# Normalising and rounding a token tile on VectorE instead of ScalarE, in the first stage of a hybrid attention kernel

## The chip, the core and the metric

The kernel runs on one core of a Trainium2 chip. The metric is the device time of one launch, in microseconds (us). The core's engines work side by side and are held together by semaphores only: TensorE (PE in the profile) for matrix products, VectorE (DVE), ScalarE (ACT), GpSimd (POOL), and SyncE (SP), which here issues the transfers.

## The reference

One layer of a diffusion backbone: 2048 sample tokens and 256 prompt tokens of width 1024, all in fp32. Every token is normalised and modulated, then projected into two mixers; their joined output is projected back, and a gated feed-forward follows.

```
h = modulate(rms_norm(x, n1), sh1, sc1)          # rms_norm: x * rsqrt(mean(x*x) + EPS) * g
qg, kg, vg, og, lr, qa, ka, va = split(h @ w_in)
o_gla = gated linear attention, forward and backward, of qg, kg, vg with gates from lr
qa, ka = rms_norm(qa, q_g), rms_norm(ka, k_g)    # and a 2-D rotary for the sample tokens
o_att = softmax attention, 8 query heads on 2 key heads, over tokens and a cache
x = x + g1 * (concat(o_gla, o_att) @ w_out)
x = x + g2 * swiglu(modulate(rms_norm(x, n2), sh2, sc2))
y = rms_norm(x, final_g)
```

## The kernel before

The kernel is a row of stages with a barrier between them: modulation parameters, `attention_projection` (names begin with `qkv_`, some 49 to 329 us), `attention` (to about 1205 us), three stages of the gated linear attention, the output projection, and the feed-forward (from about 2040 us). The change touches the class `Front`, which only `attention_projection` uses.

Every fp32 product is done as three products of halves: a value is copied in the rounded form fp32r (`hi`), the rest is `value - hi` (`lo`), and `split_product` adds hi·hi, hi·lo and lo·hi.

`attention_projection` goes over 18 tiles of 128 tokens. `steps` runs a software pipeline: in step u, `U.at(d)` gives tile u-d, and each engine does its pieces of that step in the order in which its `step` function lists them. An instruction waits with `wait_ge` on the count of a semaphore; the engine goes on with nothing else meanwhile. The path of a tile:

- `load` (SP) brings tile u as `qkv_x`, 128 x 1024. It waits for the transposes of tile u-2.
- `squares` (ACT, L255) squares and sums it. `mean` (DVE, L260) makes mean + EPS, one element per partition; `root` (POOL, L270) raises it to the power -0.5; `normalise` (ACT, L265) multiplies the tile by it, in place. All four are of tile u.
- `transpose` (PE, L277) is of tile u-1. `modulate` (ACT, L288, eight instructions) writes `qkv_hT`; `high` (ACT, L302) writes the rounded copy `qkv_hi`, `low` (DVE, L307) writes `qkv_lo`. `keep` (SP) stores `qkv_hT` for later stages.
- The products of tile u-2 with the weights (PE, 48 matrix instructions) wait for `low`.
- Of tile u-3: ACT copies the results out of PSUM (L438, L440) and squares them (L444); DVE sums the squares per head (L483, the first of its instructions in a step) and adds EPS (L485); POOL makes the root of ten elements (L533); DVE scales (L493), multiplies by a table (L499), POOL by another (L539, two instructions), DVE adds them (L502), rounds (L505, L506) and takes the rests (L508, L510).
- Of tile u-4: PE transposes the halves (L556, L558); ACT copies them out (L452, L455).

POOL's order in a step is: the two tables `qkv_cs` for tile u-3 (L530, L531: gains times rotary table, 128 x 640 each, both inputs in SBUF), L533, L539, and last `root` of tile u. Its tables for step u+1 have no input that is late, so they follow `root` of step u directly. ACT's order is: L438, L440, L444, then L452, L455, then `squares`, `modulate`, `high`, `normalise`. DVE's order is: L483 to L510, `mean`, `low`.

The weights of the stage are split once, in step 1 (L324 on ACT, L329 on DVE), behind that step's pieces.

Of the kernel before, what the change touches and what calls it, by code (L numbers as in the profile page):

```python
# [10 lines left out]
ALU = mybir.AluOpType  # L11
ACT = mybir.ActivationFunctionType
# [33 lines left out]
def wait(eng, sem, value):  # L46

    if not (isinstance(value, int) and value <= 0):
        eng.wait_ge(sem, value)
# [19 lines left out]
def steps(eng, depth, body):  # L69

    first = (depth + 2) // 2
    for u in range(2 * first):
        body(Step(u // 2, u % 2, True))
    with eng.Fori(first, N_LAT // 2) as i:
        for par in range(2):
            body(Step(i, par, False))
    for u in range(N_LAT, NT + depth):
        body(Step(u // 2, u % 2, True))
# [6 lines left out]
def bc(ap, axis, n):  # L85

    a = ap.unsqueeze(axis)
    shape = list(a.shape)
    shape[axis] = n
    return a.to_broadcast(shape)  # L90
# [137 lines left out]
class Front:  # L228
# [25 lines left out]
        wait(act, self.s.sq, t)  # L254
        act.activation(self.junk[:, :], self.x[:, par, :], ACT.Square, accum_out=self.ss[:, par, :]).then_inc(self.s.sq, 1)  # L255

    def mean(self, dve, T):
        t, half, par = T
        dve.wait_ge(self.s.sq, t + 1)
        dve.tensor_scalar(self.ms[:, par, :], self.ss[:, par, :], 1.0 / D_MODEL, EPS, ALU.mult, ALU.add).then_inc(self.s.ms, 1)  # L260

    def normalise(self, act, T):
        t, half, par = T
        act.wait_ge(self.s.rstd, t + 1)
        act.activation(self.x[:, par, :], self.x[:, par, :], ACT.Copy, scale=self.rstd[:, par, :]).then_inc(self.s.xn, 1)  # L265

    def root(self, pool, T):
        t, half, par = T
# [26 lines left out]
        sp.wait_ge(self.s.hT, t + 1)  # L295
        sp.dma_start(self.g.hT_tile(t), self.hT[:, par].rearrange("p k q -> p (k q)")).then_inc([self.s.kept0, self.s.kept1][par], 16)

    def high(self, act, T):
        t, half, par = T
        act.wait_ge(self.s.hT, t + 1)  # L300
        wait(act, self.used, t - 1)
        act.activation(self.hi[:, par], self.hT[:, par], ACT.Copy).then_inc(self.s.hi, 1)  # L302

    def low(self, dve, T):
        t, half, par = T
        dve.wait_ge(self.s.hi, t + 1)
        dve.tensor_tensor(self.lo[:, par], self.hT[:, par], self.hi[:, par].bitcast(F32), ALU.subtract).then_inc(self.s.split, 1)  # L307

# [33 lines left out]
def constant_parts(dve, parts):  # L342

    dve.memset(parts[:, :, 3, 1:HD].bitcast(F32), 0.0)
    dve.memset(parts[:, :, 3, 0:1].bitcast(F32), -1.0)


def attention_projection(nc, g):

    NH = AH + KVH  # L350
    with ExitStack() as stack:
# [5 lines left out]
        fr = Front(ph, s, g, 0, s.mkv)  # L357
# [25 lines left out]
        def key_tile(t):  # L383

            return t + 2 if cond_of(t) else t

        with nc.Block() as block:
# [41 lines left out]
            @block.scalar  # L429
            def _(act):  # L430

                def step(U):
                    if T := U.at(3):
                        t, hf, par = T
                        act.wait_ge(s.mq, t + 1)

                        wait(act, s.vlo, t - 1)
                        act.activation(qkv[:, par, 0:NQ], p_q[par][:, :], ACT.Copy).then_inc(s.eq, 1)  # L438
                        act.wait_ge(s.mkv, t + 1)
                        act.activation(qkv[:, par, NQ:D_ATT], p_kv[:, 0:D_ATT - NQ], ACT.Copy).then_inc(s.ekv, 1)  # L440
                        act.wait_ge(s.ekv, t + 1)
                        act.wait_ge(s.eq, t + 1)
                        wait(act, s.ssh, t)
                        act.activation(psq[:, :], qkv[:, par, 0:NH * HD], ACT.Square).then_inc(s.psq, 1)  # L444
                    if T := U.at(4):
                        t, hf, par = T
                        act.wait_ge(s.ptr, t + 1)
                        if isinstance(t, int) and t < 2:
                            pass
                        else:  # L450
                            act.wait_ge([s.qout0, s.qout1][par], hf * 16)
                        act.activation(qT[:, par], p_t[:, 0:AH * P].rearrange("p (h q) -> p h q", h=AH), ACT.Copy).then_inc(s.eptr, 1)  # L452
                        kt = key_tile(t)
                        col = kt * P
                        act.activation(g.keysT[:, :, :, bass.ds(col, P)],  # L455
                                       p_t[:, AH * P:(AH + 4) * P].rearrange("p (g a q) -> p g a q", g=KVH, a=2), ACT.Copy).then_inc(s.eptk, 1)
                    if T := U.at(0):
                        fr.squares(act, T)
                    if T := U.at(1):
                        fr.modulate(act, T)  # L460
                        fr.high(act, T)
                    if T := U.at(0):
                        fr.normalise(act, T)
                    if U.first(1):
                        w_act(act)

                steps(act, 4, step)
                act.wait_ge(s.eptk, NT)

            @block.vector  # L470
            def _(dve):
                constant_parts(dve, khl)
                dve.wait_ge(s.gain, 16 * 10)
                for n in range(2):
                    dve.tensor_scalar(gain[:, n, 0:AH, :], bc(gsrc[:, n, :], 1, AH), HD ** -0.5, None, ALU.mult)
                    last = dve.tensor_copy(gain[:, n, AH:NH, :], bc(gsrc[:, 2 + n, :], 1, KVH))
                last.then_inc(s.gmul, 1)

                def step(U):
                    if T := U.at(3):  # L480
                        t, hf, par = T
                        dve.wait_ge(s.psq, t + 1)
                        dve.tensor_reduce(ssh[:, :], psq[:, :].rearrange("p (h d) -> p h d", d=HD), AX.X, ALU.add).then_inc(s.ssh, 1)  # L483
                        dve.wait_ge(s.ssh, t + 1)
                        dve.tensor_scalar(msh[:, :], ssh[:, :], 1.0 / HD, EPS, ALU.mult, ALU.add).then_inc(s.msh, 1)  # L485

                        vt = key_tile(t)
                        src = qkv[:, par, NH * HD:D_ATT].rearrange("p (g d) -> p g d", g=KVH)
                        dve.wait_ge(s.ekv, t + 1)
                        v_here = g.vals[:, bass.ds(vt * KVH, KVH), :]  # L490
                        dve.tensor_copy(v_here[:, :, 0:HD], src).then_inc(s.vhi, 1)
                        dve.wait_ge(s.rsh, t + 1)
                        dve.tensor_tensor(qn[:, :, :], qkv[:, par, 0:NH * HD].rearrange("p (h d) -> p h d", d=HD),  # L493
                                          bc(rsh[:, :], 2, HD), ALU.mult).then_inc(s.qn, 1)
                        dve.wait_ge(s.vhi, t + 1)
                        dve.tensor_tensor(v_here[:, :, HD:2 * HD], src, v_here[:, :, 0:HD].bitcast(F32), ALU.subtract).then_inc(s.vlo, 1)
                        dve.wait_ge(s.qn, t + 1)
                        dve.wait_ge(s.cs, t + 1)
                        dve.tensor_tensor(m1[:, :, :], qn[:, :, :], cs[:, 0], ALU.mult).then_inc(s.m1, 1)  # L499
                        dve.wait_ge(s.m1, t + 1)  # L500
                        dve.wait_ge(s.m2, t + 1)
                        dve.tensor_tensor(rot[:, par], m1[:, :, :], m2[:, :, :], ALU.add).then_inc(s.rot, 1)  # L502
                        dve.wait_ge(s.rot, t + 1)
                        wait(dve, s.ptr, t)
                        dve.tensor_copy(qhl[:, :, 0, :], rot[:, par, 0:AH, :]).then_inc(s.hq, 1)  # L505
                        dve.tensor_copy(khl[:, :, 0:2, :], bc(rot[:, par, AH:NH, :], 2, 2)).then_inc(s.hk, 1)  # L506
                        dve.wait_ge(s.hq, t + 1)
                        dve.tensor_tensor(qhl[:, :, 1, :], rot[:, par, 0:AH, :], qhl[:, :, 0, :].bitcast(F32), ALU.subtract).then_inc(s.lo_q, 1)  # L508
                        dve.wait_ge(s.hk, t + 1)
                        dve.tensor_tensor(khl[:, :, 2, :], rot[:, par, AH:NH, :], khl[:, :, 0, :].bitcast(F32), ALU.subtract).then_inc(s.lo_k, 1)  # L510
                    if T := U.at(0):
                        fr.mean(dve, T)
                    if T := U.at(1):
                        fr.low(dve, T)
                    if U.first(1):
                        w_dve(dve)

                steps(dve, 4, step)

            @block.gpsimd  # L520
# [1862 lines left out]
```

## Time and profile before

| | |
|---|---|
| median of 3 runs | 3726.39 us (3721.03 to 3727.57) |
| profiled execution | 3721.03 us, of it 3719.1 us span in the trace |
| busy share: PE, DVE, ACT, POOL | 92%, 52%, 44%, 28% |
| stage of the change | about 49 to 329 us |

A page of the profile gives busy times and the chain that ended last; the trace behind it gives every instruction with its start, its length and what ended the idle time before it. The length of an instruction in a timeline includes any time it spends held up after its semaphores have let it go. Two instructions in a row on one engine overlap in the records by some 0.03 to 0.1 us.

### The profile page before, as it was taken

The numbers are of one execution on the slowest core, as the hardware profiler recorded it, in microseconds if no ns is written. First come the engines' busy times: TensorE is split into PE (matmuls) and PEld (weight loads), VectorE is DVE, ScalarE is ACT, GpSimd is POOL, SyncE is SP. The second block draws the span as 40 slices with busy tenths as digits, with TensorE's granted clock in tenths as the row PEclk, the third lists the DMA queues.
The fourth block names the chain that finished last, engine by engine and source line by source line (L and its number), as shares of the span: only waits on it lengthen the run. The fifth ranks groups of instructions, "written<-read, shape, count | busy, mean of one in ns | idle before, by whom it ended". The sixth has DMA issues, their size and how long they took to land. (4 is left out here: it accounts for less than half of the span.)

```text
span 3719.1 us, 48570 instructions
## 1 busy us (share of the span) xinstructions
PE 3410.6 (92%) x17904; PEld 2808.4 (76%) x17904; DVE 1944.7 (52%) x3017; ACT 1622.8 (44%) x2260; POOL 1058.2 (28%) x606
## 2 busy tenths in 40 slices
PE   5886999999997988988698899999999999999998
PEld 1774777777775886877586688888888888888897
DVE  1445999999895673338433333243334333433454
ACT  2663888888886782211244222122222222222233
POOL 0663999999995110101011000000000000000000
PEclk8997999999998998999899899999999999999999
DMA  4332111111101343336454533343334333433374
GB/s 162 118 124 86 45 42 46 45 46 42 45 24 51 132 142 117 108 103 189 143 176 169 167 92 112 103 145 98 113 99 146 99 115 99 143 100 108 120 196 147
DMA packets 383080, 405.45 MB, mean 109 GB/s; under 512 B 37476, under 2 KB 282436, under 8 KB 382916
## 3 DMA queue, kind: packets, MB, share of 16 engines
q1 hardware_dynamic: 369304, 367.18, 31.6%
q0 software_dynamic: 8432, 31.46, 2.3%
q10 hardware_dynamic: 5184, 4.72, 0.4%
q8 instruction: 95, 1.56, 0.2%
q14 instruction: 65, 0.53, 0.0%
HBM read 322.51 MB, written 80.79 MB: 108 GB/s over the span
## 5 line engine op out<-in xcount | busy, mean ns | idle before, releaser
L807 POOL TENSOR_TENSOR att_tlo<-att_prob,att_thi 128x1024 fp32r<-128x1024 f32 x292 | 693.7, 2401 | 75.8 <-ACT att_thi L976 75.8
L2134 ACT ACTIVATE ff_whi<-ff_ws 128x2048 fp32r<-128x2048 f32 (+1 forms) x170 | 317.5, 1867 | 903.5 <-PE ff_p L339 882.6
L337 PE MATMUL ff_p<-ff_hhi,ff_whi 128*128 128x512 f32 (+1 forms) x1760 | 651.2, 370 | 34.9 <-DVE ff_hlo L2190 23.3
L338 PE MATMUL ff_p<-ff_hlo,ff_whi 128*128 128x512 f32 (+1 forms) x1760 | 650.5, 370 | 0.0
L339 PE MATMUL ff_p<-ff_hhi,ff_wlo 128*128 128x512 f32 (+1 forms) x1760 | 650.4, 370 | 0.0
L2138 DVE TENSOR_TENSOR ff_wlo<-ff_ws,ff_whi 128x2048 fp32r<-128x2048 f32 (+1 forms) x170 | 378.4, 2226 | 387.6 <-ACT ff_whi L2134 387.1
L2080 POOL TENSOR_TENSOR ff_rs<-ff_ms,neg_half 128x1 f32<-128x1 f32 x18 | 9.9, 551 | 1595.9 <-DVE ff_ms L2210 1595.9
L337 PEld LDWEIGHTS ff_p<-ff_hhi,ff_whi 128*128 128x128 f32 x1760 | 334.3, 190 | 92.4 <-issue 37.3
L971 ACT ACTIVATE att_prob<-att_p_s 128x512 f32<-128x512 f32 x584 | 341.3, 592 | 101.1 <-PE att_p_s L867 94.8
L2218 DVE TENSOR_TENSOR ff_sil<-ff_sil,ff_p 128x512 f32<-128x512 f32 (+1 forms) x110 | 69.7, 633 | 589.9 <-PE ff_p L339 589.9
L339 PEld LDWEIGHTS ff_p<-ff_hhi,ff_wlo 128*128 128x128 f32 x1760 | 334.3, 190 | 55.7
L338 PEld LDWEIGHTS ff_p<-ff_hlo,ff_whi 128*128 128x128 f32 x1760 | 334.3, 190 | 54.6
L1019 DVE TENSOR_REDUCE att_mx<-att_p_r 128x1 f32<-128x512 f32 x512 | 340.8, 682 | 45.1 <-PE att_p_r L831 44.0
L976 ACT ACTIVATE att_thi<-att_prob 128x1024 fp32r<-128x1024 f32 x292 | 309.7, 1061 | 9.3
L337 PE MATMUL ff_p<-ff_whi,ff_ghi 128*128 128x512 f32 x792 | 308.2, 389 | 1.7 <-DVE ff_wlo L2138 1.7
L338 PE MATMUL ff_p<-ff_wlo,ff_ghi 128*128 128x512 f32 x792 | 308.1, 389 | 0.0
L339 PE MATMUL ff_p<-ff_whi,ff_glo 128*128 128x512 f32 x792 | 308.1, 389 | 0.0
L1046 DVE TENSOR_TENSOR att_p_sum<-att_p_sum,att_prob 128x512 f32<-128x512 f32 x420 | 290.4, 692 | 7.9
L880 PE MATMUL att_p_o<-att_thi,vals 128*128 128x512 f32 x584 | 241.1, 413 | 0.2 <-POOL att_tlo L807 0.2
L866 PE MATMUL att_p_s<-att_qa,keysT 128*128 128x512 f32 x584 | 233.3, 399 | 0.7 <-ACT att_qb L941 0.7
L881 PE MATMUL att_p_o<-att_tlo,vals 128*128 128x512 f32 x584 | 232.8, 399 | 0.0
L867 PE MATMUL att_p_s<-att_qb,keysT 128*128 128x512 f32 x584 | 231.5, 396 | 0.0
(272 smaller groups left out, 6056.7 us busy)
## 6 DMA issues: line engine op xcount, KB each, us to landing
ff_ws<-in_w_ffn_dram SPq DMA_DIRECT2D x320, 512.0 KB, 4.6
att_aw<-in_ada_w_dram SPq DMA_DIRECT2D x8, 2048.0 KB, 8.4
hT_d<-qkv_hT SPq DMA_DIRECT2D x18, 512.0 KB, 2.8
qT_d<-qkv_qT SPq DMA_DIRECT2D x18, 512.0 KB, 2.9
att_qa<-qT_d SPq DMA_DIRECT2D x36, 256.0 KB, 2.8
ga_h<-hT_d SPq DMA_DIRECT2D x18, 512.0 KB, 4.4
qkT_d<-ga_qkT SPq DMA_DIRECT2D x18, 512.0 KB, 2.9
gb_h<-hT_d SPq DMA_DIRECT2D x18, 512.0 KB, 3.4
```

The source lines that it names most:

```text
L337: pe.matmul(out, ah, bh, start=first, stop=False)
L338: pe.matmul(out, ah, bl, start=False, stop=False)
L339: return pe.matmul(out, al, bh, start=False, stop=last)
L807: pool.tensor_tensor(tlo[:, sl, :], prob[:, sl, :], thi[:, sl, :].bitcast(F32), ALU.subtract).then_inc(s.lo, 1)
L866: pe.matmul(bank[:, :], g.keysT[:, e.kv, 0, kt], qa[:, e.q, :], start=True, stop=False)
L880: pe.matmul(p_o[b.kv][:, :], v, thi[:, sl, cols], start=j == 0 and i == 0, stop=False)
L971: act.activation(prob[:, sl, i * ROW:(i + 1) * ROW], bank_of(e, j, i)[:, :], ACT.Exp).then_inc(s.ex, 1)
L976: act.activation(thi[:, sl, :], prob[:, sl, :], ACT.Copy).then_inc(s.hi, 1)
L1019: dve.tensor_reduce(mx[:, v.kv, h, c:c + 1], bank[:, :], AX.X, ALU.max).then_inc(s.mx, 1)
L1046: dve.tensor_tensor(p_sum[:, :], p_sum[:, :], half, ALU.add).then_inc(s.sum, 1)
L2134: act.activation(whi[:, par, 0:cols], ws[:, par, 0:cols], ACT.Copy).then_inc(s.w_hi, 1)
L2138: dve.tensor_tensor(wlo[:, par, 0:cols], ws[:, par, 0:cols], whi[:, par, 0:cols].bitcast(F32), ALU.subtract).then_inc(s.w_lo, 1)
```

## The change

`normalise` and the rounded copy `hi` move from ScalarE to VectorE. `mean` and `normalise` become one method on DVE, which waits for `root` of its own tile between its two instructions. `high` and `low` become `split`, also on DVE. ScalarE keeps `squares` and `modulate`. The buffers, the semaphores, and the work and order of POOL, PE and SP stay.

```diff
-    def mean(self, dve, T):
+    def normalise(self, dve, T):
         t, half, par = T
         dve.wait_ge(self.s.sq, t + 1)
         dve.tensor_scalar(self.ms[:, par, :], self.ss[:, par, :], 1.0 / D_MODEL, EPS, ALU.mult, ALU.add).then_inc(self.s.ms, 1)
-
-    def normalise(self, act, T):
-        t, half, par = T
-        act.wait_ge(self.s.rstd, t + 1)
-        act.activation(self.x[:, par, :], self.x[:, par, :], ACT.Copy, scale=self.rstd[:, par, :]).then_inc(self.s.xn, 1)
+        dve.wait_ge(self.s.rstd, t + 1)
+        dve.tensor_scalar(self.x[:, par, :], self.x[:, par, :], self.rstd[:, par, :], None, ALU.mult).then_inc(self.s.xn, 1)
...
-    def high(self, act, T):
+    def split(self, dve, T):
         t, half, par = T
-        act.wait_ge(self.s.hT, t + 1)
-        wait(act, self.used, t - 1)
-        act.activation(self.hi[:, par], self.hT[:, par], ACT.Copy).then_inc(self.s.hi, 1)
-
-    def low(self, dve, T):
-        t, half, par = T
+        dve.wait_ge(self.s.hT, t + 1)
+        wait(dve, self.used, t - 1)
+        dve.tensor_copy(self.hi[:, par], self.hT[:, par]).then_inc(self.s.hi, 1)
         dve.wait_ge(self.s.hi, t + 1)
         dve.tensor_tensor(self.lo[:, par], self.hT[:, par], self.hi[:, par].bitcast(F32), ALU.subtract).then_inc(self.s.split, 1)
...
                     if T := U.at(1):
                         fr.modulate(act, T)
-                        fr.high(act, T)
-                    if T := U.at(0):
-                        fr.normalise(act, T)
...
                     if T := U.at(0):
-                        fr.mean(dve, T)
+                        fr.normalise(dve, T)
                     if T := U.at(1):
-                        fr.low(dve, T)
+                        fr.split(dve, T)
```

## Rows read from the trace of the kernel before

**Rows 1.** The page's first part, whole kernel: busy us, share, instructions.

```profile
PE 3410.6 (92%) x17904; PEld 2808.4 (76%) x17904; DVE 1944.7 (52%) x3017; ACT 1622.8 (44%) x2260; POOL 1058.2 (28%) x606
```

**Rows 2.** Waits, 115 to 295 us: total us, times, longest.

```profile
ACT qkv_x L265 <- POOL qkv_rstd L270: 58.6, 14, 4.2
...
PE qkv_p_tr L277 <- ACT qkv_x L265: 16.4, 14, 1.2
```

**Rows 3.** Timeline, VectorE, one step: start, us, instruction, idle before it and releaser.

```profile
212.65 0.82 DVE L483 TENSOR_REDUCE qkv_ssh<-qkv_psq 128x10 f32<-128x640 f32 x1 [3.23 <-ACT qkv_psq L444]
...
220.05 0.43 DVE L505 CAST qkv_qhl<-qkv_rot 128x512 fp32r<-128x512 f32 x1
220.39 0.29 DVE L506 CAST qkv_khl<-qkv_rot 128x256 fp32r<-128x256 f32 x1
...
221.40 0.15 DVE L260 TENSOR_SCALAR qkv_ms<-qkv_ss 128x1 f32<-128x1 f32 x1
221.46 1.22 DVE L307 TENSOR_TENSOR qkv_lo<-qkv_hT,qkv_hi 128x1024 fp32r<-128x1024 f32 x1
...
225.82 0.82 DVE L483 TENSOR_REDUCE qkv_ssh<-qkv_psq 128x10 f32<-128x640 f32 x1 [3.14 <-ACT qkv_psq L444]
```

**Rows 4.** Timeline, GpSimd, the same step.

```profile
221.62 1.46 POOL L270 TENSOR_TENSOR qkv_rstd<-qkv_ms,neg_half 128x1 f32<-128x1 f32 x1 [2.54 <-DVE qkv_ms L260]
223.05 1.57 POOL L530 TENSOR_TENSOR qkv_cs<-qkv_gain,qkv_rope 128x640 f32<-128x640 f32 x1
224.57 1.61 POOL L531 TENSOR_TENSOR qkv_cs<-qkv_gain,qkv_rope 128x640 f32<-128x640 f32 x1
```

**Rows 5.** Timeline, ScalarE, the same step.

```profile
217.87 1.06 ACT L302 ACTIVATE qkv_hi<-qkv_hT 128x1024 fp32r<-128x1024 f32 x1
223.12 1.15 ACT L265 ACTIVATE qkv_x<-qkv_x,qkv_rstd 128x1024 f32<-128x1024 f32 x1 [4.19 <-POOL qkv_rstd L270]
...
225.05 0.74 ACT L444 ACTIVATE qkv_psq<-qkv_qkv 128x640 f32<-128x640 f32 x1
```

**Rows 6.** Timeline, VectorE: the first and the sixteenth L483 of the stage.

```profile
93.76 0.82 DVE L483 TENSOR_REDUCE qkv_ssh<-qkv_psq 128x10 f32<-128x640 f32 x1 [1.34 <-ACT qkv_psq L444]
...
291.78 0.82 DVE L483 TENSOR_REDUCE qkv_ssh<-qkv_psq 128x10 f32<-128x640 f32 x1 [3.15 <-ACT qkv_psq L444]
```

**Rows 7.** Timeline, GpSimd, in the warm-up: L270 while VectorE is idle.

```profile
87.55 0.55 POOL L270 TENSOR_TENSOR qkv_rstd<-qkv_ms,neg_half 128x1 f32<-128x1 f32 x1 [17.75 <-DVE qkv_ms L260]
```

**Rows 8.** Groups of instructions, VectorE, whole kernel, shapes apart: busy us, mean ns, idle before.

```profile
L1954 DVE TENSOR_SCALAR op_xn<-op_x,op_rstd 128x1024 f32<-128x1024 f32 x18 | 13.6, 753 | 21.5 <-POOL op_rstd L1855 10.8 <-PE op_p_t L1890 10.7
```

**Rows 9.** Timeline, VectorE, then GpSimd, end of the stage.

```profile
298.33 0.83 DVE L502 TENSOR_TENSOR qkv_rot<-qkv_m 128x640 f32<-128x640 f32 x1 [1.68 <-POOL qkv_m L539]
299.19 1.69 DVE L505 CAST qkv_qhl<-qkv_rot 128x512 fp32r<-128x512 f32 x1
300.80 1.62 DVE L506 CAST qkv_khl<-qkv_rot 128x256 fp32r<-128x256 f32 x1
...
298.39 2.20 POOL L530 TENSOR_TENSOR qkv_cs<-qkv_gain,qkv_rope 128x640 f32<-128x640 f32 x1 [0.17 <-POOL qkv_m L539]
300.56 1.71 POOL L531 TENSOR_TENSOR qkv_cs<-qkv_gain,qkv_rope 128x640 f32<-128x640 f32 x1
```

**Rows 10.** Timeline, GpSimd, then VectorE, in a later stage.

```profile
1261.31 1.53 POOL L1226 TENSOR_TENSOR ga_ke<-ga_qk,ga_e 128x512 f32<-128x512 f32 x1 [8.28 <-ACT ga_e L1324]
...
1261.61 1.79 DVE L1402 TENSOR_TENSOR ga_kt<-ga_qk,ga_e 128x512 f32<-128x512 f32 x1
```

**Rows 11.** Windows: length, busy of PE, PEld, DVE, ACT, POOL; PE clock; DMA.

```profile
211.14:224.32 13.18, 10.91 (x69) 9.56 (x69) 6.41 (x13) 8.85 (x18) 8.82 (x7) 1.00 0.35 124
300.00:304.00 4.00, 0.68 (x4) 0.71 (x5) 4.00 (x5) 0.85 (x2) 2.27 (x2) 0.83 0.00 0
```

**Rows 12.** Timeline, PE, in the warm-up.

```profile
92.25 1.10 PE L277 MATMUL qkv_p_tr<-ident,qkv_x 128*128 128x128 f32 x8 [2.38 <-ACT qkv_x L265]
```

## The prediction

> **What bounds the kernel now.** I read the busy shares first: PE is busy 92% of the span [rows 1]. But a stage with a barrier on both sides has its own bound, and this change lies in the first of them alone, so the share says little here. In the table of waits over the stage's steady part the reader is to see that PE waits too: 16.4 us in 14 steps for L265, and ACT waits 58.6 us for POOL's root [rows 2]. DVE in its turn stands idle for 3.23 us before L483, until ACT's L444 is done [rows 3]. Three engines that wait for each other in turn are a ring, so the next view is the timeline of one step.
>
> The ring, from L483 at 212.65 to L483 at 225.82 [rows 3]: DVE works through its chain with two waits for POOL and reaches L260 at 221.40, 8.75 us later. POOL starts its root at 221.62 and takes 1.46 us [rows 4]. ACT then normalises (223.12), copies two results out and squares them (225.05, 0.74 us) [rows 5], and DVE starts again. The first L483 is at 93.76 and the sixteenth at 291.78 [rows 6]: 15 steps of 13.20 us. PE is busy 10.9 us of such a step [rows 11], so it is not the bound: what the ring gains or loses in a step goes straight into the stage.
>
> Two things in these rows decide the case. The root takes 1.46 us in the ring but 0.55 us when DVE is idle [rows 7]: in the ring L307, a subtraction with two inputs in SBUF, has begun at 221.46 [rows 3], and POOL is held until it is nearly over. And it goes the other way: at the end of the stage the cast L505, 0.43 us elsewhere [rows 3], takes 1.69 us, and L506 takes 1.62 us instead of 0.29, because POOL's tables L530 and L531 run beside them [rows 9]. One waiting engine gets in between two instructions of the other: L531 starts its real work between L505 and L506. A subtraction or product with two SBUF inputs is held as well: L1402 takes 1.79 us beside L1226, which began 0.3 us before it [rows 10].
>
> **The change, part by part.** The order in DVE's step is now: chain, L260, wait for the root, normalise, wait for hT, round, subtract. I time it from the start of L483.
>
> Removed from the ring: ACT's normalise, and the three ACT pieces behind it. L444 now needs only PE's products and no root. PE's 10.9 us less the twenty transposes (eight take 1.10 us [rows 12], so some 2.7) leave 8.2 us for them after the subtraction has let them go. L444 follows within 1.7 us (223.12 + 1.15 to the end of L444 at 225.79 is 1.5), so it is done nearly 5 us before DVE asks. DVE's idle time in front of L483 (3.2 us a step) goes. ACT loses 1.15 + 1.06 us of work [rows 5] that was not at stake.
>
> Kept: 8.75 us to L260, 0.22 us to POOL.
>
> The root: DVE now waits for it, so the subtraction no longer holds it: 0.55 us [rows 7]. It ends at 9.52. This is a saving of 0.9 us.
>
> The normalise on DVE: not in the trace at this place, but L1954 is the same operation on the same shape, 753 ns [rows 8], against 1.15 on ACT. That is faster than an element a cycle for 1024 elements at the rate of L307 (1.22 us), so it is the same kind of instruction as L505, and can be held as L505 was. POOL's L530 follows the root at once (223.05, while the root ends at 223.08) [rows 4], 0.03 to 0.07 us ahead of what waits for the root on another engine (223.12) [rows 5]. So POOL comes first: L530 works from 9.49 to 11.06 (1.57 us). L505 ended 0.29 us after L530 (300.88 against 300.59), its own 0.43 less 0.14. The normalise then ends at 11.06 + 0.75 - 0.14 = 11.67.
>
> L531 has been waiting and gets in: in rows 9 it ended 1.39 us after the end of L505 (302.27 against 300.88). So it ends at 13.07.
>
> The rounding on DVE: the casts of 512 and 256 elements take 0.43 and 0.29 us [rows 3], so 1024 would take about 0.71 (the normalise's 0.75 is the other bound). Its input hT is there early in the step [rows 5]: L302 reads it at 217.87, 5.2 us into the step. It waits for L531 and ends at 13.07 + 0.71 - 0.14 = 13.64. The subtraction follows with 0.04 for its semaphore, 1.22 us, and ends at 14.9; the next L483 starts 0.08 us before that by the records, as L260 does behind L510. **A step is 14.82 us instead of 13.20: +1.62.** If DVE takes the first turn instead, L530 waits for the normalise, the rounding for L530, L531 for the rounding and the subtraction for L531. All the pieces are in a row again: 9.56 + 0.61 + 1.57 + 0.57 + 1.55 + 1.07, less 0.08, 14.85. Who is first hardly matters, for 3.1 us of POOL's tables and 2.4 us of DVE's work share one way.
>
> Bounds. Below: no collision at all, 9.56 + 0.67 + 0.67 + 0.04 + 1.22 less 0.04 = 12.12 us, -1.08 a step. Above: POOL keeps both turns, then normalise, rounding, subtraction: 15.05 us, +1.85 a step. I take 14.82, because rows 9 show just this pair of table instructions against this kind of instruction.
>
> At this place the Trainium skill's page "Perfetto Trace Analysis", section "Optimizing Scalar/DVE Operations", has a rule for the change: an operation that either engine can do is faster on DVE if a performance mode exists there. By that rule alone a step would be 12.12 us. The same section warns that GpSimd and DVE share a port, and the page "SBUF — State Buffer", section "Who interferes with whom", says that the one that issues first holds it for the whole instruction. Rows 9 and 10 agree with the second page, 1.69 us instead of 0.43.
>
> What waits behind DVE now. PE's transposes (L277) wait for the normalise, its products for the subtraction. In a step of 14.8 PE stands still 3.9 us in place of 2.3, in three pieces, the longest from the transposes at 11.7 to 12.8 until the subtraction is over at 14.9: 2.1 us. A pause of 2.38 us left it at speed (eight transposes in 1.10 us) [rows 12]; one of 3.6 us (DVE's L505 and L506 were held, and the transposes behind them) brought the granted clock down to a mean of 0.83 over four microseconds [rows 11]. With nearly 5 us of slack even that is hidden. SP's load of a tile waits for transposes two tiles back; it moves later by less than a step and is asked for a step after it lands. POOL is free at 13.1, before the next step begins.
>
> **The sum.** Steps 3 to 17 have all four pieces: 15 x 1.62 = +24.3 us. Warm-up: the first L483 waits 1.34 us for ACT [rows 6], which goes; with the earlier start of step 1, against a first collision, I take -1.5 (bounds 0 and -3). Step 18 has no normalise, and its tables are over before the rounding: +0.7. Steps 19 and 20 are as before, and a barrier hands the rest on. Together **+23.5 us**: 3721.0 + 23.5 = 3744.5 for the profiled execution. That one was 5.4 us under the median of its three runs, so I predict 3726.4 + 23.5 = **3750 us**, +0.63%.
>
> **Rivals.**
> 1. Faster (0.07): the collisions do not come, since DVE's new instructions do not need what POOL holds, or POOL's tables happen later. A step is 12.12: 15 x -1.08 - 3 + 0.7 = -18.5 us, 3708. For it: ACT's two instructions are each longer than DVE's. Against it: rows 9. It decides where DVE is held by POOL for less than 1.1 us a step; I count 2.7.
> 2. No change (0.08): DVE keeps both turns before POOL gets in (normalise and rounding together), and only the subtraction waits, for L530: 9.56 + 0.67 + 0.71 to 10.94, L530 until 12.37, the subtraction until 13.45, a step of 13.37. 15 x 0.17 - 2.4 + 0.7 = +1 us, 3727. Against it: L531 got in between two casts.
> 3. Much slower (0.03): PE's pauses bring it to 1.2 GHz for the whole step. Then its 10.9 us become 21.8 and PE bounds: 15 x 8.6 = +129 us, 3855. Against it: rows 12, and the clock was back at full speed soon after the pause of rows 11.
>
> **Chances.** The forecast has 0.82. A measurement of this kernel can tell about 0.2% (7.5 us) from no change: its three runs spread over 6.5 us. So slower 0.85, same 0.08, faster 0.07. The forecast's own range: a step of 14.4 us, in which one of the two casts meets less of POOL than I count, gives 15 x 1.2 - 0.8 = +17 us; the upper bound of 15.05 gives 15 x 1.85 - 0.8 = +27; the runs of one kernel spread by some 4 us around their median. So 3739 to 3758; that leaves out the three rivals, 0.18, and nothing more is needed for 8 in 10.
>
> **What would show it.** In the timeline after: root 0.55 us; normalise and rounding about 2.1 us each where 0.75 and 0.71 would be free; L531 about 2.0; no idle time of DVE in front of L483; L483 every 14.8 us; ACT waiting for PE instead of POOL; the granted clock still 1.00 in the stage; the end of the stage 23 us later, all later stages unchanged. I am wrong if the normalise is 0.75 us in the steady steps, if L483 waits for L444, or if later stages move.

## The result and the profile after

The changed kernel takes 3746.45 us (median of 4 runs, 3743.21 to 3753.3) against 3725.68 us before (4 runs, 3721.03 to 3727.57): a ratio of 1.006, 95% interval 1.0047 to 1.0073. It is slower, by 20.8 us of the medians. The profiled execution took 3746.35 us with a span of 3744.8 us, 25.7 us over the span before.

The page's first part, to be held against [rows 1]:

```profile
PE 3429.8 (92%) x17904; PEld 2819.7 (75%) x17904; DVE 2013.0 (54%) x3053; ACT 1590.0 (42%) x2224; POOL 1051.4 (28%) x606
```

DVE is busy 68 us longer and ACT 33 us less. The share says nothing on the cause: more than half of those 68 us are not work, as the next view shows.

The timeline of VectorE over one step (start, us, instruction, idle time before it and its releaser), to be held against [rows 3]:

```profile
211.65 0.81 DVE L474 TENSOR_REDUCE qkv_ssh<-qkv_psq 128x10 f32<-128x640 f32 x1
...
219.05 0.43 DVE L496 CAST qkv_qhl<-qkv_rot 128x512 fp32r<-128x512 f32 x1
219.39 0.29 DVE L497 CAST qkv_khl<-qkv_rot 128x256 fp32r<-128x256 f32 x1
...
220.40 0.15 DVE L260 TENSOR_SCALAR qkv_ms<-qkv_ss 128x1 f32<-128x1 f32 x1
221.20 2.10 DVE L262 TENSOR_SCALAR qkv_x<-qkv_x,qkv_rstd 128x1024 f32<-128x1024 f32 x1 [0.66 <-POOL qkv_rstd L267]
223.22 2.09 DVE L299 CAST qkv_hi<-qkv_hT 128x1024 fp32r<-128x1024 f32 x1
225.34 1.22 DVE L301 TENSOR_TENSOR qkv_lo<-qkv_hT,qkv_hi 128x1024 fp32r<-128x1024 f32 x1
226.49 0.81 DVE L474 TENSOR_REDUCE qkv_ssh<-qkv_psq 128x10 f32<-128x640 f32 x1
```

The same step on GpSimd, against [rows 4]:

```profile
220.62 0.55 POOL L267 TENSOR_TENSOR qkv_rstd<-qkv_ms,neg_half 128x1 f32<-128x1 f32 x1 [2.54 <-DVE qkv_ms L260]
221.16 1.58 POOL L521 TENSOR_TENSOR qkv_cs<-qkv_gain,qkv_rope 128x640 f32<-128x640 f32 x1
222.71 2.05 POOL L522 TENSOR_TENSOR qkv_cs<-qkv_gain,qkv_rope 128x640 f32<-128x640 f32 x1
```

The reader is to see three things. The root is 0.55 us now, against 1.46 in [rows 4]. The idle time of 3.23 us ahead of the reduction [rows 3] is gone: L474 follows L301 directly. And the normalise and the rounding take 2.10 and 2.09 us each. They end 0.56 us (223.30 against 222.74) and 0.55 us (225.31 against 224.76) behind the end of the table instruction beside them. From L262's start to L474's start is 5.29 us, against 2.54 in the run without tables below.

ScalarE in that step, against [rows 5]; L438 is the squaring for which L474 waits:

```profile
220.93 0.74 ACT L438 ACTIVATE qkv_psq<-qkv_qkv 128x640 f32<-128x640 f32 x1
222.45 1.02 ACT L446 ACTIVATE qkv_qT<-qkv_p_t 128x1024 fp32r<-128x1024 f32 x1 [0.78 <-PE qkv_p_t L549]
```

It is done at 221.67, 4.8 us before DVE asks. The first and the sixteenth reduction of the stage, against [rows 6]:

```profile
93.18 0.81 DVE L474 TENSOR_REDUCE qkv_ssh<-qkv_psq 128x10 f32<-128x640 f32 x1
...
315.23 0.81 DVE L474 TENSOR_REDUCE qkv_ssh<-qkv_psq 128x10 f32<-128x640 f32 x1
```

That is 15 steps of 14.80 us, against 13.20. The table of waits, 115 to 310 us (total us, times, longest), against [rows 2]:

```profile
ACT qkv_qkv L432 <- PE qkv_p_q L333: 71.1, 14, 6.6
...
PE qkv_p_q L331 <- DVE qkv_lo L301: 27.8, 13, 2.2
...
DVE qkv_x L262 <- POOL qkv_rstd L267: 8.6, 13, 0.7
PE qkv_p_tr L274 <- DVE qkv_x L262: 6.1, 6, 1.2
```

ACT no longer waits for POOL but for PE's products, which wait for DVE's subtraction. At the end of the stage the tables have run out before the rounding comes, and the same instruction is short (timeline, VectorE):

```profile
326.65 0.68 DVE L299 CAST qkv_hi<-qkv_hT 128x1024 fp32r<-128x1024 f32 x1
```

`attention` begins its first `att_prob` at 386.90 us against 362.30 before: +24.6 us from the stage. What follows it to the end of the span is 3357.9 us against 3356.8. Over all kernels of this study that rest lies between 3354 and 3364 us with no relation to the edits, so the time of a step is the sharper measure. The medians follow the start of `attention` within some 7 us, and 15 times the step within some 9.

### The profile page after: what moved, and what is told of

Read it like the earlier page. It is cut to its first block and busy times, and to the rows that moved or that the text cites. A ratio compares the mean times of both kernels' runs of the same rounds, so it can differ in the third digit from the quotient of the medians.

```text
span 3744.8 us, 48560 instructions
## 1 busy us (share of the span) xinstructions
PE 3429.8 (92%) x17904; PEld 2819.7 (75%) x17904; DVE 2013.0 (54%) x3053; ACT 1590.0 (42%) x2224; POOL 1051.4 (28%) x606
## 5 line engine op out<-in xcount | busy, mean ns | idle before, releaser
L331 PE MATMUL ff_p<-ff_hhi,ff_whi 128*128 128x512 f32 (+1 forms) x1760 | 650.0, 369 | 36.0 <-DVE ff_hlo L2181 22.8
L331 PEld LDWEIGHTS ff_p<-ff_hhi,ff_whi 128*128 128x128 f32 x1760 | 333.4, 189 | 93.7 <-issue 38.4
L331 PE MATMUL ff_p<-ff_whi,ff_ghi 128*128 128x512 f32 x792 | 308.2, 389 | 1.7 <-DVE ff_wlo L2129 1.7
```

The costliest lines, as they stand in the source:

```text
L331: pe.matmul(out, ah, bh, start=first, stop=False)
```

## The experiments

The theory: GpSimd's tables and VectorE's fast copies need the same way into SBUF, one at a time, and that costs 2.7 us of a step. Rivals: the added instructions of DVE cost this time by themselves, or by their place in the step, whatever POOL does. The step below is the distance of the first and the sixteenth reduction over 15, the ratio is to the kernel before on the same chip.

| kernel | step us | median us | ratio (95%) |
|---|---|---|---|
| before | 13.20 | 3725.2 to 3725.7 | 1 |
| changed | 14.80 | 3746.45 | 1.0060 (1.0047 to 1.0073) |
| e1 changed, tables left out | 12.08 | 3699.47 | 0.9931 (0.9915 to 0.9948) |
| e2 before, tables left out | 13.21 | 3721.01 | 0.9991 (0.9982 to 1.0001) |
| e3 normalise alone moved | 14.08 | 3733.07 | 1.0023 (1.0013 to 1.0032) |
| e4 rounding alone moved | 12.75 | 3714.33 | 0.9973 (0.9963 to 0.9983) |
| e5 changed, slower form of normalise | 14.07 | 3734.37 | 1.0029 (1.0018 to 1.0039) |
| e6 changed, rounding ahead of normalise | 13.94 | 3738.07 | 1.0036 (1.0024 to 1.0047) |
| e7 changed, small tables | 12.76 | 3710.34 | 0.9961 (0.9947 to 0.9975) |
| e9 before, early mean | 12.70 | 3716.93 | 0.9977 (0.9968 to 0.9987) |
| e10 before, small tables | 13.41 | 3723.60 | 0.9993 (0.9984 to 1.0003) |
| e8 before, both | 10.83 | 3687.67 | 0.9899 (0.9883 to 0.9916) |
| e11 changed, both | 11.90 | 3697.53 | 0.9925 (0.9908 to 0.9942) |

**Taking the tables away, in both kernels.** The edit makes `qkv_cs` in full only for the first tile; for the others one instruction of one element keeps the order and the semaphore, and the rotary of those tiles is left out. The line left out is the two instructions as they were.

```diff
-pool.tensor_tensor(cs[:, 0], gain[:, 0], bc(rope[:, par, 0, :], 1, NH), ALU.mult)
-pool.tensor_tensor(cs[:, 1], gain[:, 1], bc(rope[:, par, 1, :], 1, NH), ALU.mult).then_inc(s.cs, 1)
+if isinstance(t, int) and t == 0:
...
+else:
+    pool.tensor_tensor(cs[:, 0, 0, 0:1], gain[:, 0, 0, 0:1], rope[:, par, 0, 0:1], ALU.mult).then_inc(s.cs, 1)
```

In the changed kernel:

> The changed kernel without GpSimd's two rotary tables from the second tile on (one element is multiplied in their place, so the rotary of the later tiles is left out). Theory (VectorE's normalise and rounding are held by the two tables that GpSimd starts behind its root): normalise 0.75 us and rounding 0.7 us instead of 2.1 and 2.1, a step of 12.2 us instead of 14.8, so 15 x -2.6 = -39 us against the changed kernel, about 3707, some 18 us faster than the kernel before. Rival (VectorE simply has more to do and one more wait in a row, whoever else works): a step of 14.8 still, about 3746.

In the kernel before:

> The kernel before with the same work left out (rotary tables from the second tile on). Theory: there the tables run while VectorE is idle and waits for ScalarE, off the ring, so a step stays 13.2 us and the time 3726 within 3 us. Rival (GpSimd's load slows the stage in either kernel): the same 2 to 3 us a step are gained here as in the changed kernel, about 3690.

Measured: 12.08 and 13.21 us a step. The tables cost the changed kernel 2.72 us a step and the kernel before nothing. VectorE's timeline of the changed kernel without them:

```profile
212.57 0.76 DVE L262 TENSOR_SCALAR qkv_x<-qkv_x,qkv_rstd 128x1024 f32<-128x1024 f32 x1 [0.66 <-POOL qkv_rstd L267]
213.24 0.69 DVE L299 CAST qkv_hi<-qkv_hT 128x1024 fp32r<-128x1024 f32 x1
213.96 1.23 DVE L301 TENSOR_TENSOR qkv_lo<-qkv_hT,qkv_hi 128x1024 fp32r<-128x1024 f32 x1
```

The two instructions, in the same place and behind the same waits, take 0.76 and 0.69 us. The rival (the instructions cost this by themselves) falls. Both kernels came out 5 to 8 us below what was expected, the kernel before outside the 3 us that were given for it. The last steps explain part of it: where the tables are missing L505 and L506 aren't held either, and the last two steps take 9.9 and 10.1 us in the kernel before, in place of 12.5 and 11.4, which is 3.9 us of the 5.

**Each half of the change alone.** In the first only `normalise` is a method of DVE, `high` stays with ACT. In the second only `split` moves, and `mean` and ACT's `normalise` stay. Both cuts are told against the kernel before.

```diff
-                    if T := U.at(0):
-                        fr.normalise(act, T)
...
-                        fr.mean(dve, T)
+                        fr.normalise(dve, T)
```

> Only the normalise moves to VectorE, the rounding stays on ScalarE. Theory: normalise held by the first table until 11.7 us into the step, then the subtraction (two SBUF inputs) held by the second until 13.1, over at 14.15: a step of 14.1 us, +0.9 x 15 = +13 us, 3739. Rival (only the casts and scalings of one input are held): subtraction free, a step of 12.9, -5 us. Rival (no collision): a step of 11.5 us, -26 us, 3700.

```diff
-                        fr.high(act, T)
...
-                        fr.low(dve, T)
+                        fr.split(dve, T)
```

> Only the rounding moves to VectorE, the normalise stays on ScalarE. Theory: the rounding meets only the root (held some 0.4 us, then 0.55), ScalarE's 2.7 us behind the root stay in the ring, the subtraction is over before the tables get in: a step of 12.9 us, -4 us, 3722. Rival (each moved instruction costs its part of the +1.6 a step): half of the loss, a step of 13.9 us, +11 us.

The normalise alone, VectorE:

```profile
214.74 2.10 DVE L262 TENSOR_SCALAR qkv_x<-qkv_x,qkv_rstd 128x1024 f32<-128x1024 f32 x1 [0.66 <-POOL qkv_rstd L267]
216.76 2.61 DVE L304 TENSOR_TENSOR qkv_lo<-qkv_hT,qkv_hi 128x1024 fp32r<-128x1024 f32 x1
```

The first table holds the normalise, the second then holds the subtraction: 2.61 us in place of 1.22. So a subtraction with both inputs in SBUF is held too. The step is 14.08 us where 14.1 was expected, and the time 6 us below the 3739 expected. The rounding alone, VectorE and then GpSimd:

```profile
215.36 0.68 DVE L302 CAST qkv_hi<-qkv_hT 128x1024 fp32r<-128x1024 f32 x1
216.08 1.22 DVE L304 TENSOR_TENSOR qkv_lo<-qkv_hT,qkv_hi 128x1024 fp32r<-128x1024 f32 x1
219.19 0.82 DVE L479 TENSOR_REDUCE qkv_ssh<-qkv_psq 128x10 f32<-128x640 f32 x1 [1.89 <-ACT qkv_psq L441]
```

```profile
215.52 0.92 POOL L270 TENSOR_TENSOR qkv_rstd<-qkv_ms,neg_half 128x1 f32<-128x1 f32 x1 [2.54 <-DVE qkv_ms L260]
216.42 2.34 POOL L526 TENSOR_TENSOR qkv_cs<-qkv_gain,qkv_rope 128x640 f32<-128x640 f32 x1
```

Here DVE stays ahead of POOL, both of its instructions are free, and POOL is the one that is held: L526, 1.57 us in [rows 4], takes 2.34. The step is 0.45 us shorter than before. The root is 0.92 us, not 1.46: it gets its turn between the rounding and the subtraction, where before the subtraction stood right ahead of it, and what ACT still has to do behind it (the normalise) starts earlier. Half of the change makes the kernel faster, the other half slower, with one mechanism. Expected for it was a step of 12.9 and 3722 us; the time came out 8 us better, of which the step explains 2.

**The normalise in a slower form.** The same product, with an accumulator output that nothing reads.

```diff
-dve.tensor_scalar(self.x[:, par, :], self.x[:, par, :], self.rstd[:, par, :], None, ALU.mult).then_inc(self.s.xn, 1)
+dve.tensor_scalar(self.x[:, par, :], self.x[:, par, :], self.rstd[:, par, :], 0.0, ALU.mult, ALU.add, accum_out=self.spare[:, :]).then_inc(self.s.xn, 1)
```

> The changed kernel with VectorE's normalise in a form that also sums its results into one spare element (nothing uses it). That form takes an element a cycle, some 1.2 us instead of 0.75, so it is the slower instruction by itself. Theory (the fast form is held because it takes the second port that GpSimd's tables use; a slow form of one input is not): normalise runs beside the first table and ends at 10.9 us instead of 11.7, rounding waits for the first table only and ends at 11.7, the subtraction waits for the second table: a step of 14.1 us instead of 14.8, -11 us against the changed kernel, 3736. Rival (any VectorE instruction beside GpSimd's is held, whatever its form): a step of 15.3, +7 us, 3753.

VectorE and then GpSimd:

```profile
215.08 1.28 DVE L263 TENSOR_SCALAR_CACHE_REDUCE qkv_x<-qkv_x,qkv_rstd 128x1024 f32<-128x1024 f32 x1 [0.66 <-POOL qkv_rstd L268]
...
216.29 0.90 DVE L300 CAST qkv_hi<-qkv_hT 128x1024 fp32r<-128x1024 f32 x1
217.22 2.46 DVE L302 TENSOR_TENSOR qkv_lo<-qkv_hT,qkv_hi 128x1024 fp32r<-128x1024 f32 x1
```

```profile
215.04 1.59 POOL L522 TENSOR_TENSOR qkv_cs<-qkv_gain,qkv_rope 128x640 f32<-128x640 f32 x1
```

The slower form takes 1.28 us, about as long as a subtraction of the same size (1.22) and well over the 0.75 of the fast form, and it runs beside the table: neither holds the other (the table takes 1.59). The kernel is 12 us faster than with the fast form, which took 2.10; expected were 14.1 us a step and 3736. By this the loss hangs on the form of the instruction, not on GpSimd being busy. The Trainium skill's page "SBUF — State Buffer", section "Who interferes with whom", says just this: copies, casts and `tensor_scalar` take GpSimd's port in their two-port modes, but not in the form that also writes out its accumulator, and an instruction with two SBUF inputs meets GpSimd's reads. The rows agree on all three: 2.10 and 2.09, 1.28, and 2.46 for the subtraction L302.

**The rounding and the subtraction ahead of the normalise.** Only the order of the two pieces on DVE changes.

```diff
-                    if T := U.at(0):
-                        fr.normalise(dve, T)
                     if T := U.at(1):
                         fr.split(dve, T)
+                    if T := U.at(0):
+                        fr.normalise(dve, T)
```

> The changed kernel with VectorE's two pieces in the other order: rounding and subtraction of tile u-1 first, then mean, root and normalise of tile u. Theory: GpSimd is idle in the first pair, so they run free (0.7 and 1.2 us); only the normalise then meets the first table, and the second table runs beside the reduction L474, which has one input and is not held, but reaches into the next step and delays the root of ten elements by some 0.4 us: a step of 13.5 to 13.9 us, 14 to 20 us less than the changed kernel, about 3729. Rival (the same work in one row takes the same time in any order): 14.8, 3746.

VectorE and then GpSimd:

```profile
218.77 2.10 DVE L262 TENSOR_SCALAR qkv_x<-qkv_x,qkv_rstd 128x1024 f32<-128x1024 f32 x1 [0.66 <-POOL qkv_rstd L267]
220.78 0.81 DVE L474 TENSOR_REDUCE qkv_ssh<-qkv_psq 128x10 f32<-128x640 f32 x1
221.63 0.72 DVE L476 TENSOR_SCALAR qkv_msh<-qkv_ssh 128x10 f32<-128x10 f32 x1
```

```profile
220.22 2.10 POOL L522 TENSOR_TENSOR qkv_cs<-qkv_gain,qkv_rope 128x640 f32<-128x640 f32 x1
```

The rounding and the subtraction are free (0.69 and 1.23 us). The first table holds the normalise. The reduction L474 runs beside the second table in its full 0.81 us, but then L476, an instruction of 128 x 10 elements that takes 0.17 us in the changed kernel, takes 0.72, until L522 is done. So the step, 13.94, is just above the 13.5 to 13.9 expected, and the time 9 us above the 3729. The stage accounts for that time: the first reduction comes at 95.26, 1.5 us later than before, 15 steps are longer by 0.74, and the step after them by 1.3. `attention` starts 14.4 us later than before; the medians differ by 12.5.

**Smaller tables.** The query heads share one gain, and so do the key heads, so the tables are the same for every head of a kind. They can be made once for each kind, 128 x 256 elements in one instruction in place of twice 128 x 640, and be read by a broadcast. DVE's product becomes two instructions, POOL's two become four. The `gain` buffer is made smaller in the same way. Nothing of the computation is left out.

```diff
-        cs = ph.sb("cs", [P, 2, NH, HD])
+        cs = ph.sb("cs", [P, 2, 2, HD])
...
-                        pool.tensor_tensor(cs[:, 0], gain[:, 0], bc(rope[:, par, 0, :], 1, NH), ALU.mult)
-                        pool.tensor_tensor(cs[:, 1], gain[:, 1], bc(rope[:, par, 1, :], 1, NH), ALU.mult).then_inc(s.cs, 1)
+                        pool.tensor_tensor(cs[:, :, :, :], gain[:, :, :, :], bc(rope[:, par], 2, 2), ALU.mult).then_inc(s.cs, 1)
...
-                        dve.tensor_tensor(m1[:, :, :], qn[:, :, :], cs[:, 0], ALU.mult).then_inc(s.m1, 1)
+                        dve.tensor_tensor(m1[:, 0:AH, :], qn[:, 0:AH, :], bc(cs[:, 0, 0, :], 1, AH), ALU.mult)
+                        dve.tensor_tensor(m1[:, AH:NH, :], qn[:, AH:NH, :], bc(cs[:, 0, 1, :], 1, KVH), ALU.mult).then_inc(s.m1, 1)
```

> The changed kernel, complete, with smaller tables: the rows of the two rotary tables are the same for all query heads and for both key heads, so GpSimd makes 256 elements in one instruction instead of 1280 in two, and the products read them with a broadcast over the heads (VectorE's L490 becomes two instructions, GpSimd's pair four). Theory: the table takes 0.75 us, the normalise is held by 0.7 us and the rest is free, the four instructions cost 0.5 us more in the ring: a step of 13.2 us, -24 us against the changed kernel, 3723, no different from the kernel before. Rival (the tables' cost does not come from their length): 14.8 and more, 3750.

VectorE:

```profile
217.55 1.22 DVE L262 TENSOR_SCALAR qkv_x<-qkv_x,qkv_rstd 128x1024 f32<-128x1024 f32 x1 [0.66 <-POOL qkv_rstd L267]
218.69 0.68 DVE L299 CAST qkv_hi<-qkv_hT 128x1024 fp32r<-128x1024 f32 x1
```

The table takes 0.74 us. It holds the normalise for 0.47 us, and by the time of the rounding POOL has nothing left. The step is 12.76 where 13.2 was expected, and the time 13 us below the 3723 expected: the smaller tables give back 2.04 of the 2.72 us. With them the changed kernel is faster than the kernel before, by 0.4%.

**The mean earlier, and both.** In both kernels the ring runs through the root of tile u, although its input, ACT's sum of squares, is there long before. The second edit makes the mean while DVE waits for POOL's product, so that POOL's root follows that product directly.

```diff
+                        if T := U.at(0):
+                            fr.mean(dve, T)
                         dve.wait_ge(s.m1, t + 1)
                         dve.wait_ge(s.m2, t + 1)
...
-                    if T := U.at(0):
+                    if not U.at(3) and (T := U.at(0)):
                         fr.mean(dve, T)
```

The early mean alone, in the kernel before:

> The kernel before with the early mean alone, tables at their full length. Theory: the root runs right behind GpSimd's second product, and the two tables behind it, now beside VectorE's L502, L505 and L506, which are held as the casts were at the end of the stage before (0.4, 1.3 and 1.3 us); ScalarE drops out of the ring but VectorE's chain grows from 9.9 to 13 us: a step of 12.9 to 13.1, -3 us, 3722. Rival (the early root alone is what gained 2.4 us a step in the kernel with both edits): 10.9, 3690.

The small tables alone, in the kernel before:

> The kernel before with the smaller tables alone. Theory: the tables lie in VectorE's idle time there, so shortening them gains nothing in the ring; the four products in place of two cost 0.2 us in it: a step of 13.4 us in place of 13.2, +3 us; at the end of the stage, where the tables did hold two casts, 3 us a step come back in two steps, so -3 us in all, 3723. Rival (smaller tables alone gained 2.4 us a step): 10.9, 3690.

Both in the kernel before:

> The kernel before with the smaller tables and one move: VectorE makes mean + EPS of tile u while it waits for GpSimd's second product, so that the root follows that product and ScalarE normalises 3 us earlier. Theory (the ring of VectorE, GpSimd and ScalarE sets the stage, and the root was late for its place in VectorE's order alone): ScalarE drops out of the ring, VectorE's chain of 11.4 us is just above TensorE's 10.9: a step of 11.4 to 11.7 us, -24 us against the kernel before, 3702. Rival (the root collides with L502 and the gain is eaten): a step of 13, 3723.

Both in the changed kernel:

> The changed kernel with both edits (early mean, smaller tables), so that nothing of GpSimd runs beside VectorE's normalise and rounding. The question is whether the move is free once the collisions are gone. Theory: VectorE's chain is then 9.4 us to the subtraction, plus 0.7 for the normalise, 0.7 for the rounding and 1.15: 12.0 us a step, above TensorE's 10.9, so 15 x 1.1 = +17 us against the kernel before with the same two edits, 3704. Rival (both are then bound by TensorE): 10.9, 3688.

Alone, the early mean gives 0.50 us a step and the small tables cost 0.21 (POOL's product in four pieces is a little longer, and the tables cost the kernel before nothing, as shown above). Together they give 2.37 us. The steps of the two single edits are 12.70 and 13.41 us, where 12.9 to 13.1 and 13.4 were expected; the times are 3717 and 3724 for 3722 and 3723. VectorE with the early mean alone shows why:

```profile
216.59 1.71 DVE L507 CAST qkv_qhl<-qkv_rot 128x512 fp32r<-128x512 f32 x1
218.22 1.68 DVE L508 CAST qkv_khl<-qkv_rot 128x256 fp32r<-128x256 f32 x1
```

The tables follow the root, so an earlier root brings them into DVE's two casts, 0.43 and 0.29 us in [rows 3]. There the two are held for 2.67 us together, in every step. With small tables as well, VectorE and then GpSimd:

```profile
218.89 0.14 DVE L260 TENSOR_SCALAR qkv_ms<-qkv_ss 128x1 f32<-128x1 f32 x1
220.23 0.83 DVE L505 TENSOR_TENSOR qkv_rot<-qkv_m 128x640 f32<-128x640 f32 x1 [1.20 <-POOL qkv_m L543]
221.09 0.86 DVE L508 CAST qkv_qhl<-qkv_rot 128x512 fp32r<-128x512 f32 x1
221.87 0.28 DVE L509 CAST qkv_khl<-qkv_rot 128x256 fp32r<-128x256 f32 x1
```

```profile
220.09 0.54 POOL L270 TENSOR_TENSOR qkv_rstd<-qkv_ms,neg_half 128x1 f32<-128x1 f32 x1
220.61 1.06 POOL L533 TENSOR_TENSOR qkv_cs<-qkv_gain,qkv_rope 128x256 f32<-128x256 f32 x1
```

The mean is made in the wait for L543, the root is 0.54 us, and only the first cast is held, for 0.43 us. One step of this kernel as a window (length, busy of PE, PEld, DVE, ACT, POOL; granted clock; DMA):

```profile
205.95:216.78 10.83, 10.29 (x68) 9.22 (x67) 7.63 (x15) 8.66 (x16) 6.11 (x8) 1.00 0.38 132
```

PE is busy 10.29 us of 10.83, and over the stretch from 110 to 250 us 137.3 of 140: it is PE's own work that bounds the stage now. That was not expected: the forecast had VectorE's chain as the bound, at 11.4 to 11.7 us a step and 3702, and the time is 14 us better. The chain is shorter than it was counted. In the steps where DVE finds ACT's squares ready, as in the one from 202.88 to 213.48, a step is 10.5 to 10.7 us, so PE's bound and DVE's lie close together. This kernel is the best of all, 1.0% faster than the kernel before, and it leaves both pieces on ScalarE. The changed kernel with both edits has its normalise and rounding free (0.74 and 0.68 us), and still takes 1.07 us more a step and 9.9 us more in the median. DVE's 1.34 us lie in its ring there, while on ScalarE they are beside it. Expected was 17 us between the two, and 3704 for this one, which took 3698. The difference in the steps alone gives 15 x 1.07 = 16, of which the start of the stage gives back 2.0 (first reduction at 92.27 against 94.26), and `attention` starts 14.7 us later. What follows that start takes 3357.1 us here and 3363.9 in the other, within the spread of the rest told above; why it differs wasn't taken apart.

## Why the prediction was right

**The bound.** That a ring of DVE, POOL and ACT sets the step, not PE's 92%, holds: apart from e2, whose tables lay off the ring, every edit in e1 to e7 of a few microseconds on DVE or POOL moved the step, and only with both late edits in the kernel before did PE become the bound.

**Removed and kept.** DVE's wait of 3.23 us for ACT went, L474 to L260 stayed 8.75 us, the root went from 1.46 to 0.55. As forecast.

**The collision.** Forecast: normalise ends at 11.67 us of the step, the rounding at 13.64, the subtraction at 14.9. Measured: 11.65, 13.66 and 14.91. POOL was first after the root, by 0.04 us (221.16 against 221.20), and L522 got in between the two casts, as L531 did in [rows 9]. The step was forecast at 14.82 and is 14.80. By the rule of the Trainium skill's page "Perfetto Trace Analysis", section "Optimizing Scalar/DVE Operations", that an operation is faster on DVE where a performance mode exists, the step was worked out at 12.12 us. That is what e1 gives without the tables, 12.08; with them that rule alone gives the wrong sign.

**The sum.** 15 steps: +24.3 forecast, +24.0 measured. Warm-up: -1.5 forecast; the first reduction came 0.58 us earlier in a stage that began 0.83 us later (L466 at 64.25, its line before at 63.42, after a transfer), so -1.4. Step 18: +0.7 forecast, 13.28 against 12.50 us, +0.78. The attention starts 24.6 us later where 23.5 was forecast, 0.8 of it the late start. The medians differ by 20.8, so the 3750 us were 3.6 us too high. That is within what the rest of the kernel wanders, and 0.7 of it is the base: the median before was taken as 3726.4 and is 3725.7 over four runs.

**The rivals.** That the collisions do not come needed DVE to be held for less than 1.1 us a step: it was 2.7. The second, that DVE keeps both turns, did not come either: L522 got in between the two. In e4, where DVE waits for no root, its cast and its subtraction did stay ahead of the tables: the order depends on who is waiting for whom, as the prediction took it.

**What was wrong: the granted clock.** The step "a pause of 2.38 us left it at speed" was carried over from one row of the warm-up [rows 12]. Windows of the changed kernel, columns as in [rows 11]:

```profile
210.00:230.00 20.00, 14.57 (x79) 12.29 (x80) 13.73 (x21) 10.99 (x26) 10.44 (x7) 0.95 0.45 158
230.00:250.00 20.00, 17.82 (x95) 15.19 (x94) 13.96 (x23) 7.67 (x16) 10.80 (x8) 0.88 0.25 88
250.00:270.00 20.00, 15.22 (x102) 13.14 (x100) 15.00 (x20) 11.64 (x24) 12.54 (x9) 1.00 0.31 110
```

PE, in the step whose pause ahead of L331 was 2.10 us (timeline):

```profile
226.62 0.50 PE L331 MATMUL qkv_p_q<-qkv_w_hi,qkv_hi 128*128 128x512 f32 x1 [2.10 <-DVE qkv_lo L301]
...
227.66 0.39 PE L332 MATMUL qkv_p_q<-qkv_w_lo,qkv_hi 128*128 128x512 f32 x1
...
228.15 0.63 PE L331 MATMUL qkv_p_q<-qkv_w_hi,qkv_hi 128*128 128x512 f32 x1
```

Full speed until 227.88, then 0.63 us a matrix instruction for some 3 us: the granted clock fell to its lower level, 1.2 GHz, here 1.5 us after the pause, and came back. Before the change the clock was 1.00 in a step [rows 11]. It is below 1.00 over the steady steps of the kernels here in which instructions of DVE were held for 1.2 us or more (changed 0.94, e3 and e9 0.96, e5 and e6 0.95), and 1.00 in those where none was (e1, e2, e4, e7, e8, e10, e11). The longest pause of a step doesn't sort them: in e3 the matrix instructions took 0.63 us behind a pause of 1.44 us, while e4, with one of 1.43, stayed at 1.00. Why some steps with the same pause have it and others don't stays open. It cost nothing in the changed kernel. In the next step the products and the copies are late (ScalarE, timeline):

```profile
234.00 0.60 ACT L432 ACTIVATE qkv_qkv<-qkv_p_q 128x512 f32<-128x512 f32 x1 [6.21 <-PE qkv_p_q L333]
...
237.29 0.74 ACT L438 ACTIVATE qkv_psq<-qkv_qkv 128x640 f32<-128x640 f32 x1
```

The squaring is done at 238.03, and DVE asks at 241.28: 3.3 us of slack are left of the 4.8. In a shorter ring it does count, as e9 shows, the kernel before with the early mean. There the granted clock was 0.57 from 183 to 187 us, the squares of that step came late, and DVE waited for them (VectorE, timeline):

```profile
196.63 0.82 DVE L483 TENSOR_REDUCE qkv_ssh<-qkv_psq 128x10 f32<-128x640 f32 x1 [0.26 <-ACT qkv_psq L444]
```

That step is 12.91 us, where most of e9's are 12.56 to 12.58, and the second of its steps, with the clock at 0.57 from 104 to 112 us, is 13.70. The third rival was the far end of this.

**Left open.** Wherever the normalise ran on DVE at its place behind the root, POOL's table began 0.04 to 0.07 us ahead of it; what happens if DVE asks first after that wait wasn't tried. What makes the granted clock fall in one step and not in the next is open too.

## What to carry to other kernels

Before work is moved to a faster engine, ask what runs beside it at its new place: here 2.21 us of ScalarE became 1.45 us of VectorE and made each step 1.6 us longer, since the fast form can't run beside GpSimd's tables. A form of instruction that has two durations in one trace is a sign of it, and the cure is less work or another time for the one that holds, or a slower form that shares nothing. In a ring of engines look first for what could leave it (the early mean) and what waits behind that; the edits are worth little alone and 2.4 us a step together.

## What was not expected of the hardware

- A slower form can be the faster one: 1.28 us beside a table that held the fast form for 2.10 (e5).
- Even 128 x 10 elements are held: L476 0.72 us in place of 0.17 (e6), while the reduction of 128 x 640 just ahead of it, beside the same table, kept its 0.81.
- The holding goes both ways within one kernel: GpSimd's table of 128 x 640 took 1.57 us alone, 2.05 behind the normalise (changed), 2.34 behind the rounding and subtraction (e4).
- TensorE's granted clock fell to 1.2 GHz for some 3 us in steps whose longest pause was 2.1 us (changed) and even 1.44 us (e3), although the kernel before had kept its speed over one of 2.38 us.
